# RWKV chunks on one Trainium2 core: doubled buffers, the next super-step's setup between the inverse's levels, masks at the PSUM copy

## The chip, the cores and the metric

The kernel runs on one NeuronCore of one Trainium2 chip. The metric is the device time of one execution in microseconds (us), lower is better. All arithmetic is fp32.

## The reference

One inference step of a hybrid recurrent decoder of two layers, for a prompt of 512 tokens and eight samples of one token, width 1024. Layer 0 mixes with an RG-LRU and an RWKV-7 head group, layer 1 with SSD and GLA; both have a feed-forward part (dense, then a top-2-of-8 mixture) and a gated embedding. The change touches only RWKV-7 on the prompt: 8 heads of width 64, with a 64 x 64 state S each.

```python
def step(S, inp):
    r_t, k_t, v_t, d_t, kk_t, a_t = inp
    S = (S * d_t[:, :, None, :]
         - jnp.einsum('bhvk,bhk->bhv', S, kk_t)[..., None] * (kk_t * a_t)[:, :, None, :]
         + v_t[..., None] * k_t[:, :, None, :])
    return S, jnp.einsum('bhvk,bhk->bhv', S, r_t)

sT, y = lax.scan(step, s0.astype(jnp.float32),
                 tuple(t.swapaxes(0, 1) for t in (r, k, v, decay, kk, a)))
```

The outputs are y for every token and the last S.

## The kernel before

The program is a list of blocks, one behind the other. Inside a block each engine has its own instruction list, and the lists are tied by semaphores: w(engine, name, n) waits until the named signal has been raised n times, S(...) issues an instruction and waits for it to end. TensorE is PE, VectorE DVE, ScalarE ACT, GpSimd POOL.

The block of this case treats the 512 tokens as eight chunks of 64. The block before it has scaled each token's vectors by the running decay: rk(t, c, k, hh) is the 64 x 64 piece of kind k (RB, RK, RR, RKAP, RV) for head pair t, chunk c and head hh of the pair. The recurrence in a chunk is then a triangular system, which is solved by inverting a unit lower triangular 64 x 64 matrix per head. Two chunks form a super-step s (0 to 3), so that eight pairs of heads and chunks, n = 4 cc + t, are inverted together as 128 x 128 block-diagonal matrices.

A super-step has three stages.

- Setup: the products of RKAP and RB (L671, ps[0], copied into AL by DVE, L808), of RB/RK and RR/RKAP (L678, masked into AM by DVE, L819), the transposes of RB/RK (L686, copied to BK by ACT) and of RKAP/RV (L694, to PV by ACT). DVE makes the first mask of AL (OO, L810), the first block inverse D (DD = ident - OO, L811) and the second mask (L814). PE transposes D (L700), and ACT copies it as E.
- Inverse: five levels l, each doubling the size of the inverted blocks, for both halves cc. G = OO' E (L712); ACT copies G out of PSUM (L784); D and E products with G (L718, L719; D not in the last level); DVE subtracts them from D and E (L826, L827). POOL masks AL into OO for the next level (L658), while PE waits for it with next_o.
- Chunks: for both chunks, in order, q = RKAP' z + AM' PV (L733, L734), copied by DVE (L835) in two halves; p = E' q (L742), copied by ACT into PV (L792); the new state z from BK' PV (L750) and DVE's additions and decay (L842, L843, or L845 in chunk 0); y = z' RR + PV' AM (L759, L760), copied by ACT (L796).

All super-steps use the same buffers AL, DD, EE, GG, OO, AM, BK, PV. A super-step's setup begins when the one before has ended its D and E updates, its state z and its copies of y:

```python
for s in range(4):
    if s:
        w(pe, "de_read", 10 * s)
        w(pe, "z_read", 4 * s)
        w(pe, "y_read", 2 * s)
```

PE's matmuls of the chunks follow each other in this order, for each half, head pair and head:

```python
if c:
    pe.matmul(dst, rk(t, c, RKAP, hh), z[64 * hh:64 * hh + 64, t, :], start=True, stop=False)
mm = pe.matmul(dst, AM[:, cc, hh, t, 64:P], PV[:, hh, cc, t, :], start=c == 0, stop=True)
```

An fp32 matmul of this program stands in the trace as two records, and each has a weight load (PEld) of its own.

Of the kernel before, what the change touches and what calls it, by code (L numbers as in the profile page):

```python
# [21 lines left out]
P = 128  # L22
# [12 lines left out]
SHW = 532  # L35
# [73 lines left out]
def build_program(nc, i, o):  # L109

    with ExitStack() as ctx:
# [496 lines left out]
        AL, DD, EE, GG = [pairs(u_sb[:, n * 1024:(n + 1) * 1024]) for n in range(4)]  # L608
        OO = pairs(C[:, 0:1024])

        AM = C[:, 1024:3072].rearrange("p (c h t q) -> p c h t q", c=2, h=2, t=4)
        BK = C[:, 3072:4096].rearrange("p (h c t q) -> p h c t q", c=2, h=2, t=4)
        PV = B[:, 10240:11264].rearrange("p (h c t q) -> p h c t q", c=2, h=2, t=4)
# [4 lines left out]
        def rk(t, c, k, hh, n=1):  # L618
# [4 lines left out]
        names = ("ab_mm", "ab_read", "am_mm", "am_read", "bk_mm", "bk_read", "v_mm", "v_read", "d_ready", "e_mm",  # L623
                 "e_read", "o_ready", "next_o", "g_mm", "g_read", "eg_mm", "de_read", "q_mm", "q_read", "p_mm",
                 "p_read", "z_mm", "y_mm", "y_read", "z_read")
# [5 lines left out]
        def qz_psum(half, hh, t):  # L631

            n = 512 * half + 64 * (t % 2)
            return ps[0][64 * hh:64 * hh + 64, n:n + 64]

        def qz(half):
            return ps[0][:, 512 * half:512 * half + P].rearrange("p (t q) -> p t q", t=2)

        def nth(s, l, cc):

            return 10 * s + 2 * l + cc + 1

        with nc.Block() as block:
# [4 lines left out]
            @block.gpsimd  # L648
            def _(pool):
                S = Serial(pool, pool_step)  # L650
                pool_step.on(pool.memset(B[0:64, 10240:11264], 0.0))
                S(pool.memset(u_sb[:, 0:1024], 0.0))
                for s in range(4):
                    for l in range(4):
                        for cc in range(2):
                            n = slice(4 * cc, 4 * cc + 4)
                            w(pool, "g_mm", nth(s, l, cc))
                            g["next_o"].on(pool.tensor_tensor(OO[:, n], AL[:, n], spread(level(l + 2), 4, 1), ALU.mult))  # L658

            @block.tensor  # L660
            def _(pe):
                for s in range(4):
                    if s:
                        w(pe, "de_read", 10 * s)
                        w(pe, "z_read", 4 * s)
                        w(pe, "y_read", 2 * s)
                    for cc in range(2):
                        for t in range(4):
                            n = (4 * cc + t) * P
                            for hh in range(2):  # L670
                                mm = pe.matmul(ps[0][64 * hh:64 * hh + 64, n + 64 * hh:n + 64 * hh + 64],  # L671
                                               rk(t, 2 * s + cc, RKAP, hh), rk(t, 2 * s + cc, RB, hh),
                                               start=True, stop=True)
                    g["ab_mm"].on(mm)
                    for cc in range(2):
                        for t in range(4):
                            for hh in range(2):
                                mm = pe.matmul(ps[1 + cc][:, 512 * hh + t * P:512 * hh + (t + 1) * P],  # L678
                                               rk(t, 2 * s + cc, RB, hh, 2), rk(t, 2 * s + cc, RR, hh, 2),
                                               start=True, stop=True)  # L680
                        g["am_mm"].on(mm)
                    for cc in range(2):
                        for t in range(4):
                            for hh in range(2):
                                j, n = 64 * hh, 512 * hh + (4 * cc + t) * 64
                                mm = pe.transpose(ps[3][:, n:n + 64], rk(t, 2 * s + cc, RB, hh, 2),  # L686
                                                  ident[j:j + 64, j:j + 64])
                    g["bk_mm"].on(mm)
                    w(pe, "ab_read", s + 1)
                    for cc in range(2):  # L690
                        for t in range(4):
                            for hh in range(2):
                                j, n = 64 * hh, 512 * hh + (4 * cc + t) * 64
                                mm = pe.transpose(ps[0][:, n:n + 64], rk(t, 2 * s + cc, RKAP, hh, 2),  # L694
                                                  ident[j:j + 64, j:j + 64])
                    g["v_mm"].on(mm)
                    w(pe, "d_ready", s + 1)
                    w(pe, "am_read", 2 * s + 2)
                    for n in range(8):
                        mm = pe.transpose(ps[1][:, n * P:(n + 1) * P], DD[:, n, :], ident)  # L700
                    g["e_mm"].on(mm)
                    w(pe, "v_read", s + 1)
                    for l in range(5):
                        for cc in range(2):
                            if l == 0:
                                w(pe, "o_ready", 2 * s + cc + 1)
                                w(pe, "e_read", s + 1)
                            else:
                                w(pe, "next_o", 8 * s + 2 * (l - 1) + cc + 1)
                                w(pe, "de_read", nth(s, l - 1, cc))  # L710
                            for n in range(4 * cc, 4 * cc + 4):
                                mm = pe.matmul(ps[0][:, n * P:(n + 1) * P], OO[:, n, :], EE[:, n, :], start=True, stop=True)  # L712
# [8 lines left out]
                    w(pe, "de_read", 10 * s + 10)  # L721
                    w(pe, "bk_read", s + 1)
                    for cc in range(2):
                        c = 2 * s + cc
                        z = Zs[(c + 1) % 2]
                        for half in range(2):
                            if c:
                                w(pe, "z_read", 2 * c - 1 + half)
                            for t in (2 * half, 2 * half + 1):
                                for hh in range(2):  # L730
                                    dst = qz_psum(half, hh, t)
                                    if c:
                                        pe.matmul(dst, rk(t, c, RKAP, hh), z[64 * hh:64 * hh + 64, t, :], start=True, stop=False)  # L733
                                    mm = pe.matmul(dst, AM[:, cc, hh, t, 64:P], PV[:, hh, cc, t, :],  # L734
                                                   start=c == 0, stop=True)
                            g["q_mm"].on(mm)
                        for half in range(2):
                            w(pe, "q_read", 2 * c + half + 1)
                            for t in (2 * half, 2 * half + 1):
                                for hh in range(2):  # L740
                                    j = 64 * hh
                                    mm = pe.matmul(ps[1 + half][0:64, 512 * hh + 64 * t:512 * hh + 64 * t + 64],  # L742
                                                   EE[j:j + 64, 4 * cc + t, j:j + 64], Qs[j:j + 64, t, :],
                                                   start=True, stop=True)
                            g["p_mm"].on(mm)
                        for half in range(2):
                            w(pe, "p_read", 2 * c + half + 1)
                            for t in (2 * half, 2 * half + 1):
                                for hh in range(2):
# [1746 lines left out]
```

## Time and profile before

| | |
|---|---|
| median of 3 runs | 2452.95 us (2451.09 to 2455.77) |
| the profiled execution | 2449.99 us, span 2448.2 us |
| granted TensorE clock, mean | 0.908 |
| busy share of the span | PE 89%, PEld 78%, DVE 27%, ACT 15%, POOL 7% |
| RWKV block, first product to last copy | 219.60 to 506.28 us |

The profile shows one execution. A busy share is a mean over stages with different limits, so the stage in question is cut out of the trace below. A line of the timeline has the start and the duration of an instruction (or of several alike, x their number) in us, the engine, the line of the kernel, the operation, and what it writes and reads, with shapes; in brackets stands how long the engine had been idle before and what released it. A line of the windows has the stretch and its length in us, then for PE, PEld, DVE, ACT and POOL the busy us and the number of records, then the granted clock of TensorE (1.00 is 2.4 GHz, 0.50 is 1.2 GHz), the busy share of the DMA engines and the GB/s they moved. A group of the lines has, behind the bar, the busy us in all and the mean ns of one, then the idle time before. A busy PE need not be a PE at its peak.

### The profile page before, as it was taken

The numbers are of one execution on the slowest core, as the hardware profiler recorded it, in microseconds if no ns is written. First come the engines' busy times: TensorE is split into PE (matmuls) and PEld (weight loads), VectorE is DVE, ScalarE is ACT, GpSimd is POOL, SyncE is SP. The second block draws the span as 40 slices with busy tenths as digits, with TensorE's granted clock in tenths as the row PEclk, the third lists the DMA queues.
The fourth block names the chain that finished last, engine by engine and source line by source line (L and its number), as shares of the span: only waits on it lengthen the run. The fifth ranks groups of instructions, "written<-read, shape, count | busy, mean of one in ns | idle before, by whom it ended". The sixth has DMA issues, their size and how long they took to land. (4 is left out here: it accounts for less than half of the span.)

```text
span 2448.2 us, 32373 instructions
## 1 busy us (share of the span) xinstructions
PE 2186.0 (89%) x13264; PEld 1915.7 (78%) x13264; DVE 655.8 (27%) x1044; ACT 364.5 (15%) x678; POOL 161.0 (7%) x178
## 2 busy tenths in 40 slices
PE   6997889877899999999899877868999999999667
PEld 5876777746788888887688655758999999999656
DVE  4286332353200000003531376240000000000053
ACT  1552111110000000001122111011111111111011
POOL 0011101141300000000000200020000000000010
PEclk9998877778999999999999866968999999999878
DMA  4211000011742222222222210016777788877520
GB/s 149 69 52 43 1 1 1 1 36 47 289 177 72 73 80 84 82 65 67 82 78 69 84 52 20 18 70 227 263 255 262 262 275 277 270 252 261 196 96 35
DMA packets 74179, 293.39 MB, mean 120 GB/s; under 512 B 8577, under 2 KB 9729, under 8 KB 72817
## 3 DMA queue, kind: packets, MB, share of 16 engines
q1 hardware_dynamic: 63504, 254.95, 31.1%
q0 software_dynamic: 8256, 29.64, 3.2%
q10 hardware_dynamic: 2336, 7.62, 0.9%
q8 instruction: 61, 1.00, 0.2%
q14 instruction: 22, 0.17, 0.0%
HBM read 254.87 MB, written 37.31 MB: 119 GB/s over the span
## 5 line engine op out<-in xcount | busy, mean ns | idle before, releaser
L193 PE MATMUL ps<-normed,ring 128*128 128x260 f32 (+1 forms) x3424 | 765.0, 386 | 16.7 <-DVE normed L236 16.7
L193 PEld LDWEIGHTS ps<-normed,ring 128*128 128x128 f32 (+1 forms) x3424 | 653.9, 191 | 124.3 <-issue 22.7
L2170 PE MATMUL ps<-proj,ring 128*128 128x144 f32 x3168 | 392.6, 287 | 6.3 <-DMA ring<-in_w_moe_gu 6.3
L2170 PEld LDWEIGHTS ps<-proj,ring 128*128 128x128 f32 x3168 | 390.7, 191 | 6.8 <-issue 6.7
L2186 PE MATMUL ps<-wide,ring 128*128 128x144 f32 x1584 | 202.8, 288 | 0.0
L2186 PEld LDWEIGHTS ps<-wide,ring 128*128 128x128 f32 x1584 | 196.0, 190 | 0.9
L193 PE MATMUL ps<-proj,ring 128*128 128x260 f32 x640 | 151.5, 398 | 18.2 <-PEq L873 8.4
L193 PEld LDWEIGHTS ps<-proj,ring 128*128 128x128 f32 x640 | 127.1, 199 | 40.7 <-issue 14.0
L193 PE MATMUL ps<-wide,ring 128*128 128x260 f32 x704 | 154.6, 383 | 0.9 <-DVE wide L1182 0.9
L193 PEld LDWEIGHTS ps<-wide,ring 128*128 128x128 f32 x704 | 133.9, 190 | 21.5 <-DVE wide L1182 1.3
L2234 DVE TENSOR_TENSOR wide<-temps,ps 128x144 f32<-128x144 f32 x99 | 30.2, 305 | 397.9 <-PE ps L2170 397.9
L1182 DVE TENSOR_TENSOR wide<-temps,ps 128x520 f32 (+1 forms) x22 | 15.3, 696 | 292.0 <-PE ps L193 292.0
L211 ACT ACTIVATE temps<-resid 128x520 f32<-128x520 f32 (+1 forms) x56 | 34.6, 632 | 320.8 <-DVE resid L1191 158.3
L2239 DVE COPY proj<-ps 128x144 f32<-128x144 f32 x72 | 22.1, 308 | 211.3 <-PE ps L2186 211.3
L2205 ACT ACTIVATE temps<-ps 128x144 f32<-128x144 f32 x99 | 28.7, 290 | 290.7 <-PE ps L2170 288.4
L712 PE MATMUL ps<-normed,temps 128*128 128x128 f32 x320 | 51.2, 314 | 15.3 <-DVE normed L827 10.5
L712 PEld LDWEIGHTS ps<-normed,temps 128*128 128x128 f32 x320 | 44.9, 219 | 20.0 <-issue 19.4
L719 PE MATMUL ps<-normed 128*128 128x128 f32 x320 | 59.2, 282 | 0.0
L1161 ACT ACTIVATE temps<-ps 128x520 f32<-128x520 f32 x22 | 13.3, 604 | 294.6 <-PE ps L193 294.6
L2268 POOL DMA_INDIRECT wide<-y_slots,pos_i x10 | 11.0, 1104 | 674.4 <-DMA y_slots<-proj 671.7
L658 POOL TENSOR_TENSOR temps<-normed,phase 128x512 f32<-128x512 f32 x32 | 40.6, 1269 | 207.4 <-PE ps L712 207.4
L718 PE MATMUL ps<-normed 128*128 128x128 f32 x256 | 51.6, 285 | 0.0
(449 smaller groups left out, 1881.0 us busy)
## 6 DMA issues: line engine op xcount, KB each, us to landing
ring<-in_w_moe_gu SPq DMA_DIRECT2D x198, 512.0 KB, 4.4
ring<-in_w_moe_dn SPq DMA_DIRECT2D x72, 704.0 KB, 5.7
ring<-in_w_gu SPq DMA_DIRECT2D x44, 512.0 KB, 3.5
ring<-in_w_in_cd SPq DMA_DIRECT2D x25, 512.0 KB, 3.5
ring<-in_w_in_ab SPq DMA_DIRECT2D x22, 512.0 KB, 3.5
ring<-in_w_dn SPq DMA_DIRECT2D x16, 704.0 KB, 4.0
ring<-in_w_ple SPq DMA_DIRECT2D x16, 640.0 KB, 3.9
x_slots<-zeros POOLq DMA_DIRECT2D x19, 512.0 KB, 21.1
```

Of the source, the lines that this page charges most:

```text
L193: mm = pe.matmul(dst[0:width, a:a + HALF], slab[:, k * width:(k + 1) * width], x[:, a:a + HALF], start=first and k == 0, stop=last and k = ...
L211: act.activation(SQ_SUM if m == 0 else sq_tmp(m), h3[:, m, :] if src is None else src, ACT.Square).then_inc(sq_done.sem, 1)
L658: g["next_o"].on(pool.tensor_tensor(OO[:, n], AL[:, n], spread(level(l + 2), 4, 1), ALU.mult))
L712: mm = pe.matmul(ps[0][:, n * P:(n + 1) * P], OO[:, n, :], EE[:, n, :], start=True, stop=True)
L718: pe.matmul(ps[1][:, n * P:(n + 1) * P], GG[:, n, :], DD[:, n, :], start=True, stop=True)
L719: mm = pe.matmul(ps[2][:, n * P:(n + 1) * P], DD[:, n, :], GG[:, n, :], start=True, stop=True)
L1182: dve.tensor_tensor(dst, tmp2(m), pt(2 * (m % 2) + 1), ALU.mult).then_inc(hid_done.sem, 1)
L2170: mm = pe.matmul(hid_psum(m, s), slot(Q_MOE + 2 * m + s)[:, f * P:(f + 1) * P], XG[:, f * W:(f + 1) * W], start=f == 0, stop=f == KD - 1)
L2186: mm = pe.matmul(dn_psum(m), slot(Q_MOE + 2 * KE + m)[:, f * P:(f + 1) * P], HK(f), start=f == 0, stop=f == KE - 1)
L2205: act.activation(TMPH(m), hid_psum(m, 0), ACT.Silu).then_inc(silu_done.sem, 1)
L2234: dve.tensor_tensor(HK(m), TMPH(m), hid_psum(m, 1), ALU.mult).then_inc(hid_done.sem, 1)
L2239: dve.tensor_copy(YT[:, m * W:(m + 1) * W], dn_psum(m)).then_inc(y_kept.sem, 1)
```

## The change

- AL, D, E, AM, BK and PV have two buffers each, used by even and odd super-steps; the second ones lie in columns that the block before has finished with. GG takes the place of OO, which is gone.
- G is the product of the unmasked AL and E; the mask of the level is applied by DVE when it copies G out of PSUM (masked_g). POOL's masks for the levels go. The level masks but the first are transposed on the host.
- PE issues the setup of super-step s + 1 in pieces, one behind each level of the inverse of s: products_ab, products_am for either half, token_major for RB/RK and for RKAP/RV. The transposes of D (transpose_d) come in the second chunk, behind p. All but the first super-step's products, and the token-major transposes of RB/RK, go to ps[3].
- ACT copies AL (keep_al) and BK, PV and E as before; POOL makes D for super-steps 1 to 3; DVE masks AM at the start of levels 2 and 3.
- DVE updates E before D, and D of the second half at the next level.
- In the chunks the products with AM for q come before the state is there (value_part), behind the last level or behind p of the chunk before; the products with z follow in one group, accumulating. The y products with z come right behind those of q, those with AM behind z. q, z and p are no longer split in halves: one copy of q, one update of z, one copy of p per head of the pair.

The core of the diff, of PE's part the new order (w, rk and Serial stand above):

```diff
+        def of_head(bank, hh, t):
+            return bank[64 * hh:64 * hh + 64, 64 * t:64 * t + 64]
+        AM_HOME = lambda s, cc: ps[1 + cc] if s == 0 else ps[3]
+        BK_HOME = lambda s: ps[0] if s == 0 else ps[3]
...
+                for s in range(1, 4):
+                    w(pool, "al_read", s + 1)
+                    S(pool.tensor_tensor(DDs[s % 2], ALs[s % 2], spread(level(0), 8, 1), ALU.mult))
+                    g["d_ready"].on(pool.tensor_tensor(DDs[s % 2], spread(ident, 8, 1), DDs[s % 2], ALU.subtract))
...
+                def value_part(c):
+                    s, cc = c // 2, c % 2
+                    for t in range(4):
+                        for hh in range(2):
+                            mm = pe.matmul(of_head(q_bank, hh, t), AMs[s % 2][:, cc, hh, t, 64:P], PVs[s % 2][:, hh, cc, t, :],
+                                           start=t == 0, stop=c == 0, skip_group_check=True)
...
-                            if l == 0:
-                                w(pe, "o_ready", 2 * s + cc + 1)
+                            if l:
+                                w(pe, "ee_up", nth(s, l - 1, cc))
+                            else:
                                 w(pe, "e_read", s + 1)
-                            else:
-                                w(pe, "next_o", 8 * s + 2 * (l - 1) + cc + 1)
-                                w(pe, "de_read", nth(s, l - 1, cc))
...
+                        if l == 4:
+                            if s == 0:
+                                w(pe, "v_read", 1)
+                            value_part(2 * s)
+                        if nxt < 4:
+                            if l == 0:
...
+                                products_ab(nxt)
+                            elif l == 1:
+                                w(pe, "al_read", nxt + 1)
+                                products_am(nxt, 0)
+                            elif l == 2:
+                                w(pe, "am_read", 2 * nxt + 1)
+                                products_am(nxt, 1)
+                            elif l == 3:
+                                w(pe, "am_read", 2 * nxt + 2)
+                                token_major(nxt, BK_HOME(nxt), RB, "bk_mm")
+                            else:
+                                w(pe, "bk_read", nxt + 1)
+                                token_major(nxt, ps[3], RKAP, "v_mm")
...
+                        if c:
+                            w(pe, "z_read", c)
+                            for t in range(4):
                                 for hh in range(2):
+                                    mm = pe.matmul(of_head(q_bank, hh, t), rk(t, c, RKAP, hh), z[64 * hh:64 * hh + 64, t, :],
+                                                   start=False, stop=True, skip_group_check=True)
                             g["q_mm"].on(mm)
+                            w(pe, "y_read", c)
+                            if cc == 0 and nxt < 4:
+                                w(pe, "v_read", nxt + 1)
+                            for t in range(4):
                                 for hh in range(2):
+                                    pe.matmul(of_head(y_bank, hh, t), z[64 * hh:64 * hh + 64, t, :], rk(t, c, RR, hh),
+                                              start=t == 0, stop=False, skip_group_check=True)
+                        w(pe, "q_read", c + 1)
+                        w(pe, "ee_up", 10 * s + 10)
+                        for hh in range(2):
...
                             g["p_mm"].on(mm)
+                        if cc == 0:
+                            value_part(c + 1)
+                        elif nxt < 4:
+                            transpose_d(nxt)
...
+                    for l in range(5):
+                        if l in (2, 3):
+                            update_d(s, l - 1, 1)
+                            if s < 3:
+                                keep_am(s + 1, l - 2)
+                        masked_g(s, l, 0)
+                        if l in (1, 4):
+                            update_d(s, l - 1, 1)
+                        masked_g(s, l, 1)
+                        update_e(s, l, 0)
+                        if l < 4:
+                            update_d(s, l, 0)
+                        update_e(s, l, 1)
```

## Rows read from the trace of the kernel before

**Rows 1.** Windows of the RWKV block by stage, and their sum over twelve stages.

```profile
219.60:234.39 14.79, 8.30 (x104) 7.70 (x105) 7.66 (x8) 3.15 (x3) 1.80 (x2) 0.62 0.11 34
234.39:266.37 31.98, 28.50 (x225) 27.51 (x226) 12.38 (x18) 5.97 (x10) 10.16 (x8) 0.94 0.01 1
266.37:280.41 14.04, 12.89 (x160) 9.74 (x161) 2.92 (x10) 2.39 (x10) 0.00 (x0) 0.95 0.01 2
280.41:293.68 13.27, 8.60 (x105) 8.00 (x105) 7.66 (x8) 3.16 (x3) 0.00 (x0) 0.63 0.01 1
293.68:326.68 33.00, 29.52 (x225) 28.54 (x225) 12.36 (x18) 5.97 (x10) 10.15 (x8) 0.91 0.00 1
326.68:355.81 29.13, 28.54 (x192) 21.03 (x193) 3.51 (x12) 2.49 (x10) 0.00 (x0) 0.56 0.00 1
...
sum 286.68, PE 249.08 PEld 216.92 DVE 93.54 ACT 46.36 POOL 42.40; mean PE 20.76 PEld 18.08 DVE 7.80 ACT 3.86 POOL 3.53
```

**Rows 2.** Windows of the second super-step: inverse twice, then chunks twice.

```profile
293.70:299.00 5.30, 5.30 (x25) 5.30 (x26) 0.00 (x0) 1.19 (x2) 2.53 (x2) 0.50 0.00 0
300.00:325.00 25.00, 22.37 (x190) 21.57 (x190) 11.01 (x17) 4.78 (x8) 7.62 (x6) 1.00 0.00 1
326.00:330.00 4.00, 3.32 (x26) 2.46 (x26) 0.92 (x2) 0.00 (x0) 0.00 (x0) 1.00 0.00 0
331.00:356.00 25.00, 24.41 (x166) 18.00 (x166) 3.21 (x11) 2.49 (x10) 0.00 (x0) 0.50 0.00 1
```

**Rows 3.** Timeline of one level of the first inverse, PE and DVE.

```profile
244.41 0.39 PE L718 MATMUL ps<-normed 128*128 128x128 f32 x2
...
248.02 1.13 PE L712 MATMUL ps<-normed,temps 128*128 128x128 f32 x8
...
248.97 0.69 DVE L827 TENSOR_TENSOR normed<-normed,ps 128x512 f32<-128x512 f32 x1
...
249.81 1.13 PE L712 MATMUL ps<-normed,temps 128*128 128x128 f32 x8 [0.66 <-DVE normed L827]
...
250.77 0.39 PE L718 MATMUL ps<-normed 128*128 128x128 f32 x2
```

**Rows 4.** Timeline of PE in the chunks of the first and second super-step.

```profile
266.37 0.69 PE L734 MATMUL ps<-wide,temps 128*64 128x64 f32 x16 [0.85 <-DVE normed L827]
...
326.68 0.32 PE L733 MATMUL ps<-phase,wide 64*64 64x64 f32 x2 [0.85 <-DVE normed L827]
326.93 0.33 PE L734 MATMUL ps<-wide,temps 128*64 128x64 f32 x2
...
334.26 0.47 PE L759 MATMUL ps<-wide,phase 64*64 64x64 f32 x2
334.66 0.47 PE L760 MATMUL ps<-temps,wide 128*64 128x64 f32 x2
...
346.36 1.21 PE L742 MATMUL ps<-phase,normed 64*64 64x64 f32 x16
```

**Rows 5.** Timeline of PE in the setup of the second super-step.

```profile
280.41 1.97 PE L671 MATMUL ps<-wide 64*64 64x64 f32 x32 [0.56 <-ACT proj L796]
282.31 3.76 PE L678 MATMUL ps<-wide 64*128 64x128 f32 x32
...
290.53 1.94 PE L700 MATMUL ps<-consts,normed 128*128 128x128 f32 x8 [3.46 <-DVE temps L819]
```

**Rows 6.** Groups by line in the RWKV block.

```profile
L658 POOL TENSOR_TENSOR temps<-normed,phase 128x512 f32<-128x512 f32 x32 | 40.6, 1269 | 207.4 <-PE ps L712 207.4
...
L819 DVE TENSOR_TENSOR temps<-ps,phase 128x1024 f32<-128x1024 f32 x8 | 9.8, 1224 | 0.3
...
L835 DVE COPY phase<-ps 128x128 f32<-128x128 f32 x16 | 4.7, 292 | 53.5 <-PE ps L734 53.5
...
L776 ACT ACTIVATE wide<-ps 64x1024 f32<-64x1024 f32 x4 | 4.1, 1018 | 0.1
...
L796 ACT ACTIVATE proj<-ps 128x256 f32<-128x256 f32 x8 | 3.1, 383 | 49.3 <-PE ps L760 49.3
```

More of the change, by code:

```diff
@@ L674, in _, with products_am, token_major @@
                     g["ab_mm"].on(mm)
[L675 to L681, printed above, removed]
+                def products_am(s, cc):
+                    for t in range(4):
+                        for hh in range(2):
+                            mm = pe.matmul(AM_HOME(s, cc)[:, 512 * hh + t * P:512 * hh + (t + 1) * P],
+                                           rk(t, 2 * s + cc, RB, hh, 2), rk(t, 2 * s + cc, RR, hh, 2),
+                                           start=True, stop=True)
+                    g["am_mm"].on(mm)
+                def token_major(s, home, k, done):
                     for cc in range(2):
@@ L685, in _ @@
                                 j, n = 64 * hh, 512 * hh + (4 * cc + t) * 64
[L686 to L695, printed above, removed]
@@ new lines, in _ @@
+                products_ab(0)
+                for cc in range(2):
+                    products_am(0, cc)
+                token_major(0, BK_HOME(0), RB, "bk_mm")
+                w(pe, "al_read", 1)
+                token_major(0, ps[3], RKAP, "v_mm")
+                w(pe, "am_read", 2)
+                transpose_d(0)
+                for s in range(4):
+                    AL, DD, EE = ALs[s % 2], DDs[s % 2], EEs[s % 2]
+                    AM, BK, PV = AMs[s % 2], BKs[s % 2], PVs[s % 2]
+                    nxt = s + 1
@@ L736, in _ @@
                             g["q_mm"].on(mm)
-                        for half in range(2):
-                            w(pe, "q_read", 2 * c + half + 1)
-                            for t in (2 * half, 2 * half + 1):
+                            w(pe, "y_read", c)
+                            if cc == 0 and nxt < 4:
+                                w(pe, "v_read", nxt + 1)
+                            for t in range(4):
                                 for hh in range(2):
[L741 to L744, printed above, removed]
-                            g["p_mm"].on(mm)
@@ new lines, in _ @@
+                        w(pe, "q_read", c + 1)
+                        w(pe, "ee_up", 10 * s + 10)
+                        for hh in range(2):
+                            j = 64 * hh
+                            for t in range(4):
+                                mm = pe.matmul(ps[1][0:64, 512 * hh + 64 * t:512 * hh + 64 * t + 64],
+                                               EE[j:j + 64, 4 * cc + t, j:j + 64], Qs[j:j + 64, t, :], start=True, stop=True)
+                            g["p_mm"].on(mm)
```

234 lines of the change are left out of this document (111 added, 123 removed).

## The prediction

> **What bounds the kernel now.** I read the trace in three steps: the stretch of the RWKV chunks cut into stages, then one level of the inverse, then one chunk.
>
> Cut by stage, the RWKV block takes 286.68 us, from the first product at 219.60 to the last copy at 506.28 [rows 1]. It has four super-steps. Each is a setup (14.79 in the first, 13.27 in the second), an inverse of five levels (31.98, 33.00) and two chunks (14.04, 29.13). The third and fourth super-steps repeat the second to 0.3 us. The reader should look at two columns. PE is busy 8.60 of 13.27 us in a setup, and waits for DVE in the rest. In the second super-step's chunks PE is "busy" 28.54 of 29.13 us, so PE sets that stage by itself, although the matrices are small. DMA moves nothing to speak of in any of these stages, so no transfer is hidden behind the block and none can be late after it: what the block loses, the program loses.
>
> The granted clock is the other half [rows 2]. In the second super-step PE runs at 0.50 (1.2 GHz) for the first 5.3 us of the inverse, at 1.00 (2.4 GHz) from 300 to 325 and still in the chunks' first 4 us, and at 0.50 from 331 to 356. PE had waited for DVE for much of the time before the inverse began; in the chunks it fell while PE was issuing without a pause.
>
> One level of the inverse [rows 3] lasts 250.77 - 244.41 = 6.36 us. The 32 records of the D and E products take 248.02 - 244.41 = 3.61 us, 0.113 each. The 16 records of the G products take 1.8 at the same rate. The rest, 0.66, is a wait for DVE's E update: L827 ends at 249.66 and PE starts at 249.81, so a hand-over costs 0.15. The inverse is PE's at 85%.
>
> In a chunk the L733/L734 and L759/L760 products alternate between a 64*64 and a 128*64 tile of the array [rows 4]. At the full clock one pair of records follows the other after 0.25 us (326.93 - 326.68), at the lower after 0.40 (334.66 - 334.26). Sixteen records of one shape take 0.69 at the full clock (L734 alone) and 1.21 at the lower (L742). So sixteen alternating matmuls cost 4.1 or 6.4 us where two groups would cost 1.4 or 2.4.
>
> **The change part by part.**
>
> *Setup of steps 1 to 3 leaves the path.* That removes 3 x 13.27 = 39.8 us [rows 1]. Its PE work comes back as pieces behind the levels. Priced by [rows 5], at the inverse's full clock: products_ab 1.97 at the lower clock, so 1.0; products_am 3.76 for both, so 0.94 each; two token_major passes, 0.6 each (half of L671's records, so 0.5, and a tail). With the value part (0.7, moved out of the chunk) that is 4.8 us in each of the first three inverses. The transposes of D (L700, 1.94 at the lower clock) go between p and z of the second chunk. DVE's share of the setup goes elsewhere: the copies of AL to ACT, D to POOL, which needs 4 x 1.27 = 5.1 us [rows 6] and has from level 0 to the second chunk, some 30 us. Only the two AM masks (1.22 each) stay on DVE. ACT's copies of BK, V and AL wait for pieces, and nothing in ACT's queue but the chunk's copies stands behind them. No DMA is moved.
>
> *Masks at the PSUM copy.* ACT's copy of G becomes DVE's masked copy, priced at 0.69 like L827, which has the same size and also reads PSUM; POOL's 1.27 masks (L658, two a level) go. They were off the path: no G product waited for POOL in [rows 3]. The new level, from g(0)'s start: its eighth record ends at 1.13 (row L712), the masked copy ends at 1.85, eg(0) starts at 2.0 with the hand-over. That is 0.2 behind the last G record. Then 3.6 of D and E products: 5.6 us, and E(0), updated by 4.8, is ready before the next level. So a level costs 5.6 plus its piece, against 6.36. The last level has no D products: 1.8 + 0.2 + 1.8 = 3.8.
>
> *DVE's new queue.* It has two masked copies, two E and two D updates a level, 6 x 0.72 = 4.3 us, and in levels 2 and 3 an AM mask ahead of the masked copy. Behind E(1) at 6.6, D(1) and the mask end at 8.55, while g(0), behind its piece of 0.94 and two changes of shape, is there at 8.05: PE, waiting for the masked copy, loses 0.5 in each of the two, 1.0 a super-step.
>
> *Changes of tile shape.* A matmul that alternates costs 0.25 for its two records against 2 x 0.04 in a group, about 0.2 for the change. The pieces bring eleven changes into an inverse, 2.2 us. The lower bound is nothing, if the 0.25 comes from two products accumulating into one place; the upper is 0.28 each, from the lower clock. I take 0.2, as the shapes do differ there. The Trainium skill, "TensorEngine Tiling (Array Packing)", Key Properties, says that a change of tiling mode drains the engine. No row here separates that from the accumulation; by this rule the 2.2 us stand in each inverse, without it they go and the sum is some 7 to 10 us lower.
>
> Inverse, steps 0 to 2: 4 x 5.6 + 3.8 + 4.8 + 1.0 + 2.2 = 34.2. The start at the lower clock, 5.3 us now, loses half of that, 2.7; in step 0, where [rows 1] has 0.94 over the stage, 1.8. Step 3 has no pieces to cover the updates: g(1) waits 0.15 for E(1) at each level, and at levels 2 and 3 the masked copy another 0.5 behind D(1). That is 2 x 5.75 + 2 x 6.25 + 4.5 = 28.5, with the value part and the start 31.9.
>
> *Chunks.* Now one chain: q, copy, p, copy, z, two updates, next q. At the full clock: q 0.7; copy of 256 columns 0.42 (between 0.29 for 128, L835, and 0.69 for 512); p 1.0; ACT copy 0.38 (L796); z 0.7; two updates 0.84; hand-overs 0.7. That is 4.7. At the lower clock q and z are 1.2 each. p runs four heads on one tile in a row: 1.2 (L742) if that overlaps as now, 1.7 if weight load and product follow each other as for L700 (0.24 a record, half the columns); I take 1.7 with 0.2 for its tail. That makes 6.7. The y products with z lie behind the copy of q; those with the values behind the updates of z. In the first chunk the value part costs 0.2 beyond the p copies, in the second the transposes 1.1 (0.3 at the full clock). The next inverse needs no z and follows the y products. Two chunks: 9.8 full, 14.6 lower. Steps 1 to 3 start at the full clock and fall after 4 us as now: 13.0. Where a super-step begins its chunks, the V copy (L776, 1.02 on ACT) holds the y products and through them p: 0.5; the changes of shape on the path: 0.8. Step 0's first chunk has no state: 3.3, its second 5.0 at the full clock, in all 8.5 with a change.
>
> *First setup.* AL goes to ACT after the load, D follows on DVE, then the AM masks. Two masks (L814, the size of L827, 0.7 each) leave DVE: 14.8 becomes 13.3.
>
> **Sum.** Step 0: 13.3 + 36.0 + 8.5 = 57.8. Steps 1 and 2: 36.9 + 13.0 + 1.3 = 51.2 each. Step 3, which has neither the V copy nor the transposes but ends with the copy of y: 31.9 + 13.0 + 0.5 = 45.4. In all 205.6 against 286.7: 81 us less. The profiled execution took 2449.99 (span 2448.2), so it would take 2369; it lay 3 below the median of the runs, 2452.95. I forecast 2371 us, between the two.
>
> **The rivals.**
>
> *The clock stays up in the chunks* and so at the starts of the inverses. For it: step 0's chunks ran at 0.95 to their end nearly [rows 1]. Against: the three others fell after 4 us, and the new chunks have PE waiting half of the time. Time: three stages of 9.8 for 13.0 and three starts of 2.7 less, 18 us: 2353.
>
> *The regrouping doesn't do what it says*: an accumulating 64*64 product costs its 0.25 or 0.40 in a group too. Then q and y cost 3.2 each instead of 1.2 at the lower clock, 0.6 of it hidden: 3.4 us in each of seven chunks, 24 us: 2395. Against: L734 and L742 in groups [rows 4], though neither accumulates.
>
> *DVE becomes the bound of the inverse.* Its 4.3 us a level wait on PE in program order; where a D or E update stands ahead of a masked copy that PE needs, PE idles. If that is 1.7 us more a level, with 20 levels, 34 us: 2405. For it: it is 0.5 in two levels by my own count; against: updates and masks alternate so that each has PE work behind it.
>
> *Slower: the lower clock spreads over the inverse.* The pieces of small tiles could take the granted clock down there, as the chunks do now. PE's 32 us of work at the full clock in each of the first three inverses (25 in the last) would double. The sum becomes 13.3 + 3 x 66 + 54 + 9 + 3 x 15.4 = 320, 33 us over before: 2486. It decides from the point where about 80 of the 120 us of that work run at 1.2 GHz. Against: the inverse held 1.00 from 300 to 325 with a wait in each level [rows 2], and it now has fewer.
>
> **How the numbers follow.** The forecast has 0.60, the clock staying up 0.13, the regrouping in vain 0.09, DVE as the bound 0.12, the slower case 0.04; 0.02 is left for a mixture that ends at no change. A measurement of this kernel tells 0.2%, about 5 us, from no change. Faster 0.94, same 0.02, slower 0.04. The forecast's own bounds are the unknown prices: changes of shape at nothing (-10), p overlapping (-4), against 0.28 a change (+3), 0.15 more at each of the some 60 hand-overs on the path (+9) and chunks wholly at the lower clock (+5). That is 2357 to 2388 for it alone; the range takes in the first two rivals with a margin for their own bounds: 2345 to 2402.
>
> **What would show it.** The block's stages: about 36, 37, 37 and 32 for the inverses, 13 for a pair of chunks, nothing between. In the chunks the L733 and L759 successors come as groups of sixteen records in 0.7 to 1.2 us. In the inverse, PE's idle time before D and E products is 0.2 a level and 0.7 in levels 2 and 3; if more, DVE is the bound. The granted clock by stage decides the first and the last rival. The forecast is wrong if a group of accumulating products is no faster than the alternation, or if the inverse runs at 0.50.

## The result, and the profile after

The changed kernel takes 2343.4 us in the median of four runs (2342.7 to 2345.43); the kernel before, on the same chip, 2453.73 (2451.09 to 2455.77). The ratio is 0.9552, 95% interval 0.9536 to 0.9569: 110 us less. 2371 was forecast, so the direction was right, the size was 28 us too small, and the time lies just below the range, beyond the rival in which the clock stays up (2353). The profiled execution took 2345.43 (span 2343.6, mean granted clock 0.929).

The windows by stage answer to [rows 1]; the columns are the same. In order: first setup; inverse and chunks of super-steps 0, 1, 2, 3.

```profile
220.41:233.34 12.93, 8.75 (x105) 8.09 (x105) 4.81 (x4) 4.34 (x5) 3.54 (x3) 0.63 0.12 39
233.34:268.57 35.23, 33.93 (x336) 31.88 (x337) 22.14 (x31) 2.31 (x4) 4.72 (x2) 0.96 0.01 2
268.57:276.04 7.47, 6.95 (x153) 6.12 (x153) 1.23 (x3) 3.72 (x7) 0.00 (x0) 1.00 0.01 2
276.04:309.91 33.87, 32.62 (x337) 30.48 (x337) 22.18 (x32) 2.68 (x4) 4.72 (x2) 1.00 0.00 1
309.91:319.17 9.26, 7.92 (x189) 7.09 (x185) 2.08 (x5) 3.75 (x7) 0.00 (x0) 1.00 0.02 4
319.17:353.04 33.87, 32.62 (x336) 30.49 (x336) 22.20 (x32) 2.68 (x4) 4.72 (x2) 1.00 0.01 2
353.04:362.30 9.26, 7.92 (x188) 7.09 (x185) 2.08 (x5) 3.75 (x7) 0.00 (x0) 1.00 0.01 2
362.30:390.90 28.60, 27.74 (x241) 26.24 (x241) 19.49 (x30) 0.38 (x1) 0.00 (x0) 1.00 0.01 1
390.90:399.63 8.73, 6.99 (x180) 6.23 (x176) 2.69 (x7) 2.09 (x6) 0.00 (x0) 1.00 0.01 2
sum 179.22, PE 165.43 PEld 153.73 DVE 98.90 ACT 25.71 POOL 17.70; mean PE 18.38 PEld 17.08 DVE 10.99 ACT 2.86 POOL 1.97
```

The block takes 179.22 us where it took 286.68. (The span is shorter by 104.6: the block starts 0.8 later, and what follows it takes 1944.0 instead of 1941.9.) By stage, with the third and fourth super-steps of before from the same trace (inverses 32.92 and 32.69, chunks 29.14 and 29.18):

| us | before | forecast | after |
|---|---|---|---|
| setups on the path | 54.6 | 13.3 | 12.9 |
| four inverses | 130.6 | 141.7 | 131.6 |
| four pairs of chunks | 101.5 | 50.6 | 34.7 |

Of the 107.5 us that the block gained, 66.8 lie in the chunks. The inverses took in three setups' PE work and are only 1 us longer than before. The column to look at is the granted clock, the last but two: 0.63 in the first setup and 0.96 in the first inverse, much as before, then 1.00 in every stage, where [rows 2] has 0.50 in the chunks and at the start of the inverse.

PE's timeline of the second super-step: level 0 (with the piece L676 behind it), the waits of levels 2 to 4, and both chunks.

```profile
276.04 2.05 PE L733 MATMUL ps<-proj,normed 128*128 128x128 f32 x16
278.05 0.49 PE L739 MATMUL ps<-normed,temps 128*128 128x128 f32 x2
...
281.50 0.39 PE L740 MATMUL ps<-temps,normed 128*128 128x128 f32 x2
281.82 1.15 PE L676 MATMUL ps<-wide 64*64 64x64 f32 x32
282.90 2.05 PE L733 MATMUL ps<-proj,normed 128*128 128x128 f32 x16
...
292.30 0.49 PE L739 MATMUL ps<-normed,temps 128*128 128x128 f32 x2 [0.48 <-DVE temps L862]
...
299.70 0.49 PE L739 MATMUL ps<-normed,temps 128*128 128x128 f32 x2 [0.48 <-DVE temps L862]
...
307.56 1.16 PE L740 MATMUL ps<-temps,normed 128*128 128x128 f32 x8 [0.29 <-DVE temps L862]
...
309.91 0.68 PE L772 MATMUL ps<-phase,wide 64*64 64x64 f32 x16
311.18 0.68 PE L780 MATMUL ps<-wide,phase 64*64 64x64 f32 x16 [0.59 <-ACT wide L823]
311.67 0.91 PE L787 MATMUL ps<-phase,proj 64*64 64x64 f32 x16
...
314.79 0.68 PE L772 MATMUL ps<-phase,wide 64*64 64x64 f32 x16 [0.59 <-DVE phase L906]
315.30 0.63 PE L780 MATMUL ps<-wide,phase 64*64 64x64 f32 x16
316.07 0.96 PE L787 MATMUL ps<-phase,proj 64*64 64x64 f32 x16
316.96 1.09 PE L700 MATMUL ps<-consts,normed 128*128 128x128 f32 x8
...
319.17 2.05 PE L733 MATMUL ps<-proj,normed 128*128 128x128 f32 x16
```

A level takes 281.82 - 276.04 = 5.78 us, and its piece 1.08. In levels 2 and 3 PE stands idle for 0.48 us, waiting for the masked copy (L862), and for 0.29 in the last level. The products that alternated in [rows 4] stand in groups of sixteen records: L780 follows by 0.49 in front of L787, 0.031 a record. One chunk takes 4.88 (314.79 - 309.91), the next 4.38.

### The profile page after: what moved, and what is told of

It is laid out like the page before. It is cut to its first block and busy times, and to the rows that moved or that the text cites. A ratio compares the mean times of both kernels' runs of the same rounds, so it can differ in the third digit from the quotient of the medians.

```text
span 2343.6 us, 32272 instructions
## 1 busy us (share of the span) xinstructions
PE 2104.6 (90%) x13264; PEld 1855.1 (79%) x13264; DVE 661.3 (28%) x1039; ACT 343.8 (15%) x630; POOL 136.8 (6%) x153
## 5 line engine op out<-in xcount | busy, mean ns | idle before, releaser
L740 PE MATMUL ps<-temps,normed 128*128 128x128 f32 x320 | 58.8, 278 | 1.1 <-DVE temps L862 1.1
L1224 ACT ACTIVATE temps<-ps 128x520 f32<-128x520 f32 x22 | 13.3, 604 | 295.0 <-PE ps L193 295.0
L740 PEld LDWEIGHTS ps<-temps,normed 128*128 128x128 f32 x320 | 46.6, 192 | 2.4 <-DVE temps L862 2.2
L193 PE MATMUL ps<-temps,consts 128*128 128x260 f32 x28 | 12.5, 592 | 39.2 <-PEq L265 16.1
L1254 DVE TENSOR_TENSOR resid<-ps,resid 128x520 f32 (+1 forms) x8 | 5.6, 700 | 146.8 <-PE ps L193 146.8
```

The costliest lines, as they stand in the source:

```text
L193: mm = pe.matmul(dst[0:width, a:a + HALF], slab[:, k * width:(k + 1) * width], x[:, a:a + HALF], start=first and k == 0, stop=last and k = ...
L740: mm = pe.matmul(ps[2][:, n * P:(n + 1) * P], DD[:, n, :], GG[:, n, :], start=True, stop=True)
L1224: act.activation(tmp2(m), pt(2 * (m % 2)), ACT.Silu).then_inc(silu_done.sem, 1)
```

## Experiments

All medians are set against the kernel before on the same chip (2453.5 to 2454.7).

### The two halves apart: e1 and e2

e1 is the changed kernel with the alternation of before in its chunks, so that the products with AM no longer come ahead of the state; e2 is the kernel before with only the regrouping. Core of e1 (y likewise):

```diff
+                        for t in range(4):
+                            for hh in range(2):
+                                if c:
+                                    pe.matmul(of_head(q_bank, hh, t), rk(t, c, RKAP, hh), z[64 * hh:64 * hh + 64, t, :],
+                                              start=True, stop=False)
+                                mm = pe.matmul(of_head(q_bank, hh, t), AM[:, cc, hh, t, 64:P], PV[:, hh, cc, t, :],
+                                               start=c == 0, stop=True)
```

Core of e2, where the z products formed one alternating loop with the AM products:

```diff
+                            if c:
+                                for t in (2 * half, 2 * half + 1):
+                                    for hh in range(2):
+                                        pe.matmul(qz_psum(half, hh, t), rk(t, c, RKAP, hh), z[64 * hh:64 * hh + 64, t, :],
+                                                  start=t == 2 * half, stop=False, skip_group_check=True)
```

> The changed kernel with only the regrouping of the chunks undone: the products of q with z and with AM, and those of y, alternate head by head again (64*64, 128*64), accumulating; pipeline, masks and buffers stay. Theory 'sparse products': the granted clock fell in the old chunks because the alternation spreads few products over a long time; then it falls here too. Chunk pairs of super-steps 1 to 3 at 0.50 to 0.60 and about 31 us (9.3 in the changed kernel), the first levels of the next inverse at 0.50 (2.7 us more each), in all about 2420 us. Rival 'waits of the setup': the clock fell because PE waited for DVE in each setup, which the pipeline ended; then it stays at 1.00 here, the alternation costs its 4.1 us a group, chunk pairs about 22 us, in all about 2388.

> The kernel before with the regrouping alone: in the chunks the products with z come as a group and then those with AM or PV, in q for each half, in y for all heads; setups, buffers and masks as before. Sparse products: the chunks stay at 1.00, pairs of super-steps 1 to 3 fall from 29.1 to about 10, the first from 14.0 to 7.6, in all about 64 us less: 2390; the setups still run at 0.5 to 0.63 and the inverses start at 0.50. Waits of the setup: the chunks fall to 0.50 after 4 us as before, pairs about 14, in all 2402.

e1: 2427.91 us (ratio 0.9898, 0.9881 to 0.9914), 26 less than before. e2: 2384.88 (0.9724, 0.9707 to 0.974), 69 less. Together they would give 95; the whole change gives 110, so 15 come only with both. Windows of e1: a pair of chunks split after its first 4 us, and the start of the next inverse.

```profile
318.87:322.87 4.00, 4.00 (x36) 2.99 (x32) 0.22 (x1) 1.02 (x1) 0.00 (x0) 1.00 0.01 4
323.00:348.00 25.00, 23.27 (x164) 17.64 (x164) 2.54 (x6) 2.83 (x6) 0.00 (x0) 0.59 0.00 1
...
348.73:353.00 4.27, 4.27 (x25) 4.27 (x25) 1.25 (x2) 0.38 (x1) 0.00 (x0) 0.62 0.00 0
```

Windows of e2: a pair of chunks, the next setup, the start of the next inverse.

```profile
320.84:330.20 9.36, 9.02 (x192) 7.18 (x192) 3.49 (x12) 2.11 (x9) 0.00 (x0) 1.00 0.01 2
330.76:343.20 12.44, 6.06 (x105) 5.52 (x105) 7.65 (x8) 3.16 (x3) 0.00 (x0) 0.87 0.01 1
343.20:348.00 4.80, 4.80 (x27) 4.80 (x28) 0.00 (x0) 1.19 (x2) 2.24 (x2) 0.62 0.00 0
```

PE in the setup of super-step 1 in e2, at the transposes of D (the next setup's wait is the same to 0.01 us):

```profile
286.08 1.94 PE L700 MATMUL ps<-consts,normed 128*128 128x128 f32 x8 [5.18 <-DVE temps L824]
```

With the alternation the clock falls after the first 4 us, as in [rows 2], though no setup stands ahead of these chunks; grouped, it stays at 1.00 in the kernel before too, and the pair takes 330.76 - 320.84 = 9.92 us up to the next setup, instead of 29.13. So the fall in the chunks belongs to the alternation and not to the setup's waits. In e2 PE still waits 5.18 us for DVE in a setup, and the inverse behind it starts at 0.62; in the changed kernel, without the setup between, it starts at 1.00.

By stage, from the start times in the four profiled executions:

| us | before | e1 | e2 | changed |
|---|---|---|---|---|
| setups on the path | 54.6 | 12.9 | 51.9 | 12.9 |
| four inverses | 130.6 | 133.4 | 128.3 | 131.6 |
| four pairs of chunks | 101.5 | 110.0 | 38.0 | 34.7 |

What comes only with both halves lies mostly in the chunks, not at the starts of the inverses (those of e1 lack the value part, 0.6 each). With the alternation in place, the rest of the change makes the chunks 8.5 us longer; with the products grouped, it makes them 3.3 us shorter. The chunks took in the transposes of D and the wait for the V copy, and their copies are no longer split in halves; which of these costs more beside the alternation was not tested. In these executions 8.6 us come only with both, 15 by the medians; e1's profiled execution, 2423.67, is 4 us below its median.

### Shape or accumulation: e3, e3g, e5

The alternation of before changed the tile's shape at every matmul and also accumulated two products into one place. e3 alternates y's z products (64\*64) with the new state's (128\*64), which go to different banks and accumulate nothing between them. e3g puts the same products at the same point in two groups. e5 keeps one shape, and issues each z product of q twice in a row.

```diff
# e3
                             for hh in range(2):
+                                if c:
+                                    pe.matmul(of_head(y_bank, hh, t), z[64 * hh:64 * hh + 64, t, :], rk(t, c, RR, hh),
+                                              start=t == 0, stop=False, skip_group_check=True)
                                 mm = pe.matmul(of_head(z_bank, hh, t), BK[:, hh, cc, t, :], PV[:, hh, cc, t, :],
# e5
+                                    for _ in range(2):
+                                        mm = pe.matmul(of_head(q_bank, hh, t), rk(t, c, RKAP, hh),
+                                                       z[64 * hh:64 * hh + 64, t, :], start=False, stop=True,
+                                                       skip_group_check=True)
```

> The changed kernel, with the products of y with z (64*64) moved behind p and alternating there with those of the new z (128*64). The two go to different PSUM banks, so no two neighbours accumulate into one place; only the tile shape changes 16 times in a group of 32 records. If the shape change is what the alternation costs: 0.25 a matmul, 4.1 us for the sixteen instead of 1.1, some 3 us in each of seven chunks, about 2362 us or more if the clock falls. If it is the accumulation into one place: within 5 us of 2343.

> The control of the kernel in which y's products with z alternate with those of the new z: the same place behind p, but one group behind the other. What differs between the two is the 15 changes of shape in each of seven chunks. Expected: 0.5 us a chunk more than the changed kernel, because the group no longer lies behind the copy of q: about 2347, at 1.00 throughout. If the move itself cost the 30 us, about 2370.

> The changed kernel with each of the products of q with z issued twice in a row into the same place (the values of q count double, so the output is another; the work is otherwise the same). All have one shape. If back-to-back accumulation into one place costs 0.25 a matmul, each group takes 4.1 instead of 0.52: 3.6 us in seven chunks, about 2368. If it costs nothing, eight more matmuls of 0.065 each: 0.5 a chunk, about 2347.

Two runs each: e3 2374.47 us (2369.8 to 2379.13), e3g 2350.47 (2350.37 to 2350.57), e5 2345.58 (2345.13 to 2346.03). PE's timelines of e3, e3g and e5, in this order:

```profile
273.72 0.32 PE L795 MATMUL ps<-wide,phase 64*64 64x64 f32 x2
273.98 0.33 PE L797 MATMUL ps<-wide,temps 128*64 128x64 f32 x2
274.23 0.33 PE L795 MATMUL ps<-wide,phase 64*64 64x64 f32 x2
```

```profile
275.69 0.68 PE L795 MATMUL ps<-wide,phase 64*64 64x64 f32 x16
276.30 0.69 PE L799 MATMUL ps<-wide,temps 128*64 128x64 f32 x16
```

```profile
309.84 1.20 PE L773 MATMUL ps<-phase,wide 64*64 64x64 f32 x32
```

Alternating, a matmul comes every 0.26 us, as in [rows 4], without any accumulation. Grouped, sixteen records follow by 0.61 and the next sixteen by 0.52. Accumulating without a change of shape, 32 records take 1.20 us, 1.20 / 32 = 0.038 or less each. So the 0.26 goes with the change of shape, and accumulation costs nothing that shows. The Trainium skill, "TensorEngine Tiling (Array Packing)", Key Properties, says that changing the tiling mode drains the engine; e3 and e5 agree in that a change costs time, though no run shows the drain itself. The price is 0.26 for a matmul that alternates against 0.065 in a group. At the one boundary behind a long group the price is smaller, about 0.1: the last D and E pair above starts at 281.50, a pair takes 0.22, and the next shape starts at 281.82.

e3 is 24 us above e3g, and part of that is the clock again. Windows of e3: chunks of super-steps 1 and 2 (part of the pair).

```profile
314.00:328.50 14.50, 13.33 (x166) 10.60 (x163) 2.10 (x5) 3.12 (x7) 0.00 (x0) 1.00 0.00 1
363.00:383.00 20.00, 19.02 (x171) 15.18 (x172) 2.15 (x6) 3.21 (x7) 0.00 (x0) 0.64 0.00 1
```

With half of the alternation, the clock held in one super-step and fell in another of the same execution; the two runs of e3 lie 9 us apart.

### Do waits alone bring the clock down? e4

The copy of q is made seven times, so that PE waits longer in every chunk; no product alternates.

```diff
+                        for _ in range(6):
+                            S(dve.tensor_copy(Qs, four(q_bank)))
                         S(dve.tensor_copy(Qs, four(q_bank)), g["q_read"])
```

> The changed kernel with the copy of q made seven times instead of once (0.45 us each), so that PE waits 2.7 us longer in each of the eight chunks. Sparse products: what counts is the alternation, so the clock holds at 1.00 and the cost is 8 x 2.7 = 21.6 us, about 2365. If waits of PE bring the clock down as the alternation does, the chunk pairs (14.7 us) run partly at 0.50 and the inverses start there: another 3 x (3 + 2.7), about 2382.

2377.46 us (2374.26 to 2380.67; two runs), between the 2365 worked out for a clock that holds and the 2382 for one that falls. The window of a pair of chunks in e4, then PE's timeline in it:

```profile
318.98:336.55 17.57, 12.13 (x189) 10.92 (x185) 7.08 (x17) 3.93 (x7) 0.00 (x0) 0.71 0.01 2
```

```profile
323.01 1.60 PE L787 MATMUL ps<-phase,proj 64*64 64x64 f32 x16 [2.07 <-DVE phase L904]
...
332.02 1.16 PE L787 MATMUL ps<-phase,proj 64*64 64x64 f32 x16 [2.58 <-DVE phase L904]
```

The clock fell. My theory after e1 and e2, that only the alternation brings it down, was too narrow: with waits of 2.07 and 2.58 us in its chunks, and no alternation, it falls too; with waits of 0.59, in the changed kernel, it does not. The inverse behind these chunks runs at 1.00 again.

### DVE's order in the inverse: e6, e7, e8, e9

At levels 2 and 3 the AM mask (1.22 us) stands ahead of the masked copies that PE needs. e6 moves it behind them:

```diff
-                        if l in (2, 3):
-                            update_d(s, l - 1, 1)
-                            if s < 3:
-                                keep_am(s + 1, l - 2)
                         masked_g(s, l, 0)
-                        if l in (1, 4):
+                        if l:
                             update_d(s, l - 1, 1)
                         masked_g(s, l, 1)
+                        if l in (2, 3) and s < 3:
+                            keep_am(s + 1, l - 2)
```

e7 leaves DVE as it is and moves all pieces of PE between the G products and the D and E products, to cover the wait for the masked copy; e8 does both.

```diff
# e7: the loop of the D and E products, and value_part, go behind the pieces
                             g["g_mm"].on(mm)
-                        for cc in range(2):
-                            w(pe, "g_read", nth(s, l, cc))
...
                         if nxt < 4:
...
+                        for cc in range(2):
+                            w(pe, "g_read", nth(s, l, cc))
```

> The changed kernel with the AM masks of levels 2 and 3 behind both masked copies of G instead of ahead of them, and D of the second half between the copies at every level. If DVE's order costs what the prediction counted, the wait of 0.5 before the D and E products of levels 2 and 3 goes: 2 x 0.5 in three super-steps, some more in the fourth, 3 to 4 us: 2340. If the mask only moves the wait to E, the time stays at 2343.

> The changed kernel with the pieces of the next setup between the G products and the D and E products of their level, instead of behind these. They then fill PE's wait for the masked copy (0.2 at each of four levels, 0.5 at the last), and the V copy ends before the chunks (0.6): some 1.8 us in each of three super-steps, 5 us, about 2338. Against it: behind the D and E products the next G products then wait for E (0.15 a level), which would leave 3 us: 2340.

> Both of the two edits: AM masks behind the masked copies, pieces ahead of the D and E products. If they add up, 7 to 9 us less than the changed kernel, about 2335; if each only shifts the same wait, about 2339.

e6: 2339.16 us (ratio 0.9532, 0.9517 to 0.9546). This interval overlaps that of the changed kernel (0.9536 to 0.9569), so the 4 us rest on the trace: the level waits of 0.48 are gone, and the second super-step runs from 275.78 to 317.87, 42.09 us where the changed kernel has 43.13. e7 missed: 2347.62 (0.9563, 0.9548 to 0.9577), which cannot be told from the changed kernel. e8 missed by far: 2365.89 (0.9644, 0.9631 to 0.9658). PE's timelines of e7, then of e8:

```profile
294.39 1.16 PE L684 MATMUL ps<-wide 64*128 64x128 f32 x16 [0.82 <-DVE temps L857]
...
302.15 0.71 PE L694 MATMUL ps<-consts,wide 64*128 64x64 f32 x16 [0.82 <-DVE temps L857]
```

```profile
301.29 1.16 PE L684 MATMUL ps<-wide 64*128 64x128 f32 x16 [2.44 <-DVE temps L857]
...
312.31 0.71 PE L694 MATMUL ps<-consts,wide 64*128 64x64 f32 x16 [2.45 <-DVE temps L857]
```

L857 is the AM mask. A piece waits until the mask of the piece before it has emptied the bank. Behind the D and E products the piece had 3.6 us of cover; ahead of them it has none, and it waits for the mask while the D and E products, which are ready, queue behind it. In e8 the mask itself stands behind both masked copies, and the wait triples. Windows of e8, around the first of these waits:

```profile
296.00:300.00 4.00, 2.85 (x24) 2.51 (x22) 3.33 (x5) 0.00 (x0) 0.00 (x0) 1.00 0.00 0
300.00:304.00 4.00, 2.71 (x25) 2.59 (x26) 1.22 (x1) 0.00 (x0) 0.00 (x0) 0.86 0.00 0
304.00:308.00 4.00, 4.00 (x28) 4.00 (x27) 1.41 (x3) 0.00 (x0) 0.00 (x0) 0.71 0.02 4
```

Behind the wait the clock falls, inside an inverse, where a pair of D and E records then follows the next by 0.43 us instead of 0.22, up to 306.35. That is the mechanism of the slower rival, on a small scale and set off by a wait, not by small tiles.

e9 keeps e6's order, puts the transposes of V (which no mask holds up) ahead of the last level's D and E products, and splits the transposes of D in two halves, one at the start of the second chunk:

```diff
+                        if l == 4 and nxt < 4:
+                            w(pe, "bk_read", nxt + 1)
+                            token_major(nxt, ps[3], RKAP, "v_mm")
...
+                        if cc and nxt < 4:
+                            transpose_d(nxt, 0, 4)
...
-                            transpose_d(nxt)
+                            transpose_d(nxt, 4, 8)
```

> The changed kernel with three orders changed: AM masks behind the masked copies (measured: 4 us less); in the last level the transposes of V ahead of the D and E products, where PE waits 0.5 and the V copy then holds nothing back (0.6), 1.1 us in three super-steps; the transposes of D in two halves, one in PE's 0.6 wait for z and one behind p, 0.5 in three super-steps. In all 8 us less than the changed kernel: 2335. Rival: the wait at 0.6 before q is needed for the order of the copies too, so that only the first two count: 2337; or the split adds changes of tile shape at 0.1 and gives nothing.

2337.18 us in five runs (2336.41 to 2338.93), ratio 0.952 (0.9507 to 0.9533): the best of all, 6 us below the changed kernel by the medians, 8 by the ratios, as expected; its interval lies clear of the changed kernel's but not of e6's. The three orders were not tried one by one. The second super-step takes 40.63 us (274.76 to 315.39), where e6 has 42.09. Windows of its second inverse and chunks:

```profile
274.76:306.76 32.00, 32.00 (x332) 30.23 (x334) 21.70 (x32) 3.70 (x5) 4.72 (x2) 1.00 0.01 2
306.76:315.39 8.63, 8.34 (x196) 7.25 (x191) 2.57 (x6) 2.74 (x6) 0.00 (x0) 1.00 0.01 2
```

PE shows no idle time in this inverse and 0.29 us in the chunks. What remains is set by PE itself, though its busy time still holds the changes of shape.

### The masks alone: e10

The kernel before, with only the masks moved to the PSUM copy (POOL's masks and ACT's copies of G gone):

```diff
-                            g["next_o"].on(pool.tensor_tensor(OO[:, n], AL[:, n], spread(level(l + 2), 4, 1), ALU.mult))
...
+                            S(dve.tensor_tensor(GG[:, n], pairs(ps[0][:, 512 * cc:512 * cc + 512]),
+                                                spread(level(l + 1), 4, 1), ALU.mult), g["g_read"])
```

> The kernel before with the masks at the PSUM copy alone: G is made from the unmasked AL, DVE masks it on the way out of PSUM, ACT's copies of G and POOL's masks go, DVE's two masks in each setup go. If PE sets the inverse, nothing is gained there; four setups lose 1.4 us each, because the AM masks end that much earlier: 5.7 less than before, about 2448. If POOL's masks had been the limit of the inverse, 20 levels would gain 0.6 each as well: 2436.

2442.08 us (ratio 0.9945, 0.993 to 0.996), 12.6 less than before, between the two values expected, so the stages have to decide. Windows of e10: first setup, first inverse, second setup.

```profile
220.34:233.44 13.10, 8.70 (x104) 8.10 (x105) 6.28 (x6) 3.16 (x3) 1.79 (x2) 0.63 0.11 39
233.44:265.29 31.85, 28.13 (x224) 27.02 (x224) 19.30 (x28) 0.00 (x0) 0.00 (x0) 0.95 0.00 1
279.73:290.67 10.94, 7.19 (x104) 6.76 (x105) 6.27 (x6) 3.16 (x3) 0.00 (x0) 0.80 0.01 1
```

The inverse hardly moves (31.85, 31.98 in [rows 1]): the 0.6 a level that POOL's masks would have held, 3 us here, is not there. The setups do: 13.10 for 14.79, 10.94 for 13.27. The first is the 1.4 of two masks that left DVE; in the second PE also waits less and is granted 0.80 instead of 0.63. These four, 1.7 + 3 x 2.3 = 8.7, are most of the gain. The second inverse is 1.3 us shorter (31.73), as its first 5.33 us run at 0.68 instead of 0.50; the fourth, which starts at 0.50, is not (32.86).

## Why the prediction was right, and where it was wrong

These steps held. The setup of steps 1 to 3 left the path, and the queues it was moved into held PE up as counted: 0.59 for the V copy, summed at 0.5. The inverse is PE's: 33.87 us where 34.2 was summed, with a level of 5.78 for 5.6 to 6.0 with its changes of shape. The first setup is 12.9 for 13.3. DVE's new queue cost what was worked out, a wait of 0.48 in levels 2 and 3, and e6 got it back. POOL's masks were off the path, as read from [rows 3] and shown by e10. Changes of shape, not accumulation, made the alternation slow (e3, e5), and the regrouping does what it says (e2). The rivals "regrouping in vain", "DVE as the bound" and "slower" fall: e5 refutes the first; PE is busy 32.62 of 33.87 us in the inverse, against the second; the clock is 1.00 there, against the third.

The step that failed is in *Chunks*: "Steps 1 to 3 start at the full clock and fall after 4 us as now: 13.0". The fall was read from [rows 2] and carried over to chunks that no longer did what had preceded it. With it came the 2.7 us of each inverse's start, though the setup ahead of it was gone. What the runs showed instead: alternating, the clock falls (e1); grouped, it holds, in the new kernel and in the old one (e2): a pair of chunks took 9.26 us at 1.00, not 13.0. The rival "the clock stays up" named this, and had 0.13 because the old chunks were "busy" and the new ones wait: I took PE's busy column for work. A pair of alternating records lasts 0.26 us in the trace where a grouped one needs 0.065, so a busy share of 98% there was mostly change of shape.

The block was forecast at 205.6 and took 179.2, 26.4 us less. The pairs of chunks account for 50.6 - 34.7 = 15.9. By the forecast's own prices the clock is 3 x (13.0 - 9.8) = 9.6 of it. The other 6.3 is a second step that failed, the price of the chunks at the full clock: a pair of step 1 or 2 would have been 9.8 + 1.3 = 11.1, and took 9.26 with the V copy's wait and the transposes in it. The groups of q and z were summed at 0.7, the time that a group shows with the end of its last record; the next group follows by 0.51 (314.79 to 315.30). For p 0.89 was measured (316.07 to 316.96) and 1.0 summed, for a change of shape about 0.1 and 0.2.

The inverses account for 141.7 - 131.6 = 10.1, of it 3 x 2.7 = 8.1 for starts that no longer come at the lower clock. The 2 us left are a balance: eleven changes of shape at about 0.1 gave back more, and the last level, summed at 3.8, took 4.54 (304.11 to 308.65). The first setup gave 0.4. So 9.6 + 8.1 = 17.7 of the 26.4 us are the clock, as the rival priced it, and the rest are terms summed too long.

Open stays what exactly brings the clock down. Shown: alternation does, with waits of no more than 0.6 us beside it (e1); waits of 2 to 2.6 us do without it (e4, e8); half of the alternation does in one super-step and not in another (e3); grouped small products with waits of 0.59 do not, nor do the waits of 0.82 in e7. Alternation doesn't always do it at once: in step 0 of the kernel before it began at 269.43, and the clock was 1.00 up to 278. Chunks whose products all have one tile shape were not tried.

## What to carry to other kernels

Before a low clock is carried into a forecast, ask what PE did before it fell, and whether the change leaves that standing: here that carried 17.7 of the 26.4 us by which the block's forecast was too long. A PE that shows busy on small matrices is to be measured by the distance of its records, not by its busy share; where two tile shapes alternate, group them first, which alone took 69 us off here (e2). When work is moved to cover a wait, look for what the moved work itself waits for, since everything behind it in the queue then waits too (e7, e8).

## What the hardware showed unexpectedly

A change of tile shape costs 0.19 us when every matmul makes one (0.26 for 0.065), but about 0.1 behind a long group. Accumulating twice in a row into one place costs nothing visible (1.20 us for 32 records).

The granted clock fell while PE showed 4.00 of 4.00 and then 23.27 of 25.00 us busy (e1). The Trainium skill, "TensorE: Matmul & The Clock Gate", Part 1, says that the gate goes by how busy PE has been; by the profile's busy column e1 doesn't agree, while e4 and e8, where it fell with waits of 2 us and more, do.
